# Starting a layer's first products on half of its row tiles, and moving turned tiles between PSUM banks

## The reference

```python
for i in range(DEPTH):                       # block 2, DEPTH = 2
    last = i == DEPTH - 1
    hx = rmsnorm_2(x, g_pre_mix[i]) * (1.0 + sc1) + sh1
    hc = rmsnorm_2(ctx, g_pre_mix[i]) * (1.0 + csc1) + csh1
    px = hx @ w_in[i]                        # q, k, v, Fourier part, 3 Hyena parts
    pc = hc @ (w_in[i][:, K0:F0] if last else w_in[i])
    ...                                      # attention of q over [kc, k], [vc, v]
    hy_x = hyena_mix(px[..., H0:], w_hy_conv[i], b_hy_conv[i], filt, hy_bias[i])
    mix_x = jnp.concatenate([attn_x, four_x, hy_x], axis=-1) @ w_out[i]
    x = x + ga1 * rmsnorm_2(mix_x, g_post_mix[i])
    ...                                      # the same for ctx, only if not last
    fx = rmsnorm_2(x, g_pre_ffn[i]) * (1.0 + sc2) + sh2
    x = x + ga2 * rmsnorm_2(conv_ffn_2(fx, ...), g_post_ffn[i])
    ...                                      # the same for ctx, only if not last
```

## Time and profile before

| | us |
|---|---|
| median of 3 runs | 1617.51 (1617.08 to 1620.24) |
| the profiled execution, its own time | 1620.15 |
| its span in the trace | 1618.3 |
| granted clock of TensorE, mean | 0.996 |
| PE busy | 1573.3 |
| DVE busy | 1114.7 |
| ACT busy | 832.2 |
| POOL busy | 276.6 |

### The profile page before, as it was taken

How to read it: one execution, slowest core, us unless ns; L and a number is a source line. 1 busy time by engine, 2 the same in 40 slices (tenths; PEclk the granted TensorE clock), 3 DMA queues, 4 the chain that set the end, 5 groups by cost and what they waited for, 6 DMA issues and landing times.

```text
span 1618.3 us, 22543 instructions
## 1 busy us (share of the span) xinstructions
PE 1573.3 (97%) x8459; PEld 1270.3 (78%) x8459; DVE 1114.7 (69%) x1830; ACT 832.2 (51%) x1524; POOL 276.6 (17%) x336
## 2 busy tenths in 40 slices
PE   8999999999999999999989999999999999999998
PEld 7667888887677888878857788888888886788886
DVE  5686899656877999755775745444533587689974
ACT  5556666545555666542355533333411544667653
POOL 2000011810003111900010001111272001001163
PEclk9999999999999999999999999999999999999999
DMA  8556866555579654652264433332232346656652
GB/s 274 182 175 194 225 188 182 188 185 169 192 259 255 172 157 156 207 183 85 79 244 122 138 109 93 104 102 82 103 131 97 101 147 207 174 154 183 191 197 80
DMA packets 267349, 261.72 MB, mean 162 GB/s; under 512 B 9025, under 2 KB 209009, under 8 KB 266602
## 3 DMA queue, kind: packets, MB, share of 16 engines
q1 hardware_dynamic: 262986, 246.15, 49.6%
q0 software_dynamic: 3968, 13.82, 2.5%
q10 hardware_dynamic: 288, 0.33, 0.1%
HBM read 259.12 MB, written 1.13 MB: 161 GB/s over the span
## 4 chain that ended last, share of the span: by engine, by line
PE 81%; DVE 11%; ACT 4%; DMA 2%; issue 2%; SPq 0%; DVEq 0%; ACTq 0%
PE psv L584 58%; PE pss L584 20%; DVE wL L1368 2%; PE pss L634 2%; DMA ring<-in_w_up 1%; ACT scr L2206 1%; PE psv L634 1%; ACT wH L2063 1%; DVE scr L1564 1%; DVE hHL L1439 1%; DMA ring<-in_w_in 1%; DVE scr L1565 1%; DVE mx L1530 1%; ACT scr L2063 0%; DVE W L1430 0%
## 5 line engine op out<-in xcount | busy, mean ns | idle before, releaser
L584 PE MATMUL psv<-hHL,wH 128*128 128x512 f32 (+1 forms) x1952 | 641.1, 391 | 6.5 <-DVE hHL L1439 3.4
L1368 DVE TENSOR_TENSOR wL<-ring,wH 128x1024 fp32r<-128x1024 f32 (+2 forms) x364 | 454.9, 1254 | 212.4 <-ACT wH L2063 209.4
L2063 ACT ACTIVATE wH<-ring 128x1024 fp32r<-128x1024 f32 (+2 forms) x364 | 377.0, 1040 | 256.0 <-PE psv L584 200.8
L584 PE MATMUL psv<-hHL,wL 128*128 128x256 f32 (+1 forms) x1504 | 466.3, 310 | 0.0
L584 PEld LDWEIGHTS psv<-hHL,wH 128*128 128x128 f32 x1952 | 364.0, 188 | 91.6 <-DVE wL L1368 7.5
L584 PE MATMUL psv<-wH,hHL 128*128 128x512 f32 (+3 forms) x872 | 293.4, 386 | 4.8 <-DVE wL L1368 2.5
L584 PEld LDWEIGHTS psv<-hHL,wL 128*128 128x128 f32 x1504 | 284.5, 189 | 15.7
L584 PE MATMUL pss<-wH,hHL 128*128 128x512 f32 (+3 forms) x872 | 291.6, 384 | 1.3 <-ACT scr L2063 1.0
L584 PEld LDWEIGHTS psv<-wH,hHL 128*128 128x128 f32 x872 | 162.9, 188 | 43.0 <-DVE wL L1368 9.3
L584 PEld LDWEIGHTS pss<-wH,hHL 128*128 128x128 f32 x872 | 163.0, 188 | 34.3 <-issue 2.3
L1157 POOL TENSOR_TENSOR W<-scr 128x256 f32<-128x256 f32 (+1 forms) x88 | 82.4, 937 | 563.2 <-ACT scr L2268 563.2
(11 more groups left out here) (280 smaller groups left out, 1606.0 us busy)
## 6 DMA issues: line engine op xcount, KB each, us to landing
ring<-in_w_up SPq DMA_DIRECT2D x176, 512.0 KB, 5.2
ring<-in_w_mod SPq DMA_DIRECT2D x96, 512.0 KB, 4.8
ring<-in_w_down SPq DMA_DIRECT2D x88, 512.0 KB, 4.3
ring<-in_w_in SPq DMA_DIRECT2D x52, 512.0 KB, 4.6
ring<-in_w_out SPq DMA_DIRECT2D x32, 512.0 KB, 5.1
ring<-in_w_in SPq DMA_DIRECT2D x8, 384.0 KB, 6.1
W<-gate_scratch POOLq DMA_DIRECT2D x3, 1024.0 KB, 7.6
ring<-in_w_in SPq DMA_DIRECT2D x8, 288.0 KB, 6.6
```

The source lines that it names most:

```text
L584: return pe.matmul(o, a, b, start=start, stop=stop, skip_group_check=True)
L1368: v.tensor_tensor(lo, raw, hi.bitcast(F32), ALU.subtract).then_inc(piece_split, told("piece_split", p))
L2063: return ac.activation(o, i, ACT.Copy)
```

## The change

There are three parts.

**The context follows later.** At the end of block 2's first layer `transition()` gives way to `context_later()`, on DVE and on ACT. Only tiles 0 and 1 are brought to the end before the Hyena pieces. Tile 0 is turned inside the last down products of tile 3, tile 1 right behind them; there is no `keep_clock`. The residuals and the normalising of tiles 2 and 3, their squares, their turns and parts, and the modulation column run between the Hyena pieces (`context_features`, `context_squares`). The context's gain row has a tile of its own, `gain_ctx`, that POOL loads with one DMA of 512 KB.

**pT in the V banks.** In block 2's attention the turned probabilities go to PSV instead of PSS. ACT and DVE get waits that keep the order of the rotation.

**By halves.** All V halves of the low parts are made first, then all S halves, so that the next products can begin with the V half's features while the S halves are still made; ACT makes the high parts in a matching order. One tile before each product stage (tile 1, or tile 3 before the first layer's FFN of block 2) is normalised in two operations of 512, and its V half is turned after the first. In the two-tile transition the first weight split stands ahead of tile 1's gate.

```diff
@@ -640 +646 @@
+    def normalised(ph, t, k0):
+        if t == halved(ph) and k0 == 0:
+            pe.wait_ge(rows_normalised, at("rows_normalised", ph, t, "half"))
+        else:
+            pe.wait_ge(rows_normalised, at("rows_normalised", ph, t))
     def feature_tile(ph, t, x, banks=None):
...
-        pe.wait_ge(rows_normalised, at("rows_normalised", ph, t))
         for (kind, b), k0 in zip(banks or feature_banks(ph, t), (0, 4)):
+            normalised(ph, t, k0)
             for k in range(4):
@@ -777 +791 @@
                 two = (2 * p - 4, 2 * p - 3)
-                pe.wait_ge(S_free, at("S_free", ph, "pT", two[1]))
+                pe.wait_ge(FREE[turned], at(turned + "_free", ph, "pT", two[1]))
                 b = open_("V", ph, "pv", two[1])
@@ -789 +803 @@
                     pe.wait_ge(probs_ready, at("probs_ready", ph, i))
-                    transposes("S", (ph, "pT", i), [(probs(i)[:, c * P:(c + 1) * P], slice(c * P, c * P + P)) for c in range(4)])
+                    transposes(turned, (ph, "pT", i), [(probs(i)[:, c * P:(c + 1) * P], slice(c * P, c * P + P)) for c in range(4)])
             if p - 1 in mods:
@@ -901 +915 @@
             kind = "VS"[t % 2]
+            if (ph, t, h, j) == (("b2", 0), 3, 1, NJ - PIECES):
+                feature_tile(("b2", 1, "mix"), 0, xn4[:, 0, :])
             if j == 0:
@@ -1000 +1016 @@
         pe.wait_ge(pick_made, 5)
-        to_features2(ph + ("mix",), range(4 if l else NT), MOD2[l - 1]["end"] if l else MOD2[l]["start"], (0, 6, 0, 2) if l else (0, 4))
+        if last:
+            feature_tile(ph + ("mix",), 1, xn4[:, 1, :])
+            modulation_row(1, MOD2[0]["end"][0], "S")
+        else:
+            to_features2(ph + ("mix",), range(NT), MOD2[l]["start"], (0, 4))
         def hyena_columns(s):
@@ -1026 +1046 @@
-        for m in HY:
-            tile_split(ntok, ph, "hy", m, head=(ph + ("mix",), 3 if l else 1) if m == HY[0] else None)
+        for i, m in enumerate(HY):
+            tile_split(ntok, ph, "hy", m, head=(ph + ("mix",), 1) if m == HY[0] else None)
+            if last and i == 0:
+                modulation_col(1, MOD2[0]["end"][0], "S")
             if m == 0:
...
                     hyena_columns(s)
+            if last and i >= 4:
+                feature_tile(ph + ("mix",), i - 2, xn4[:, i - 2, :])
         hyena_forward(0)
@@ -1038 +1062 @@
             hyena_forward(1)
+        if last:
+            pe.wait_ge(V_free, at("V_free", ph + ("mix",), "hT", 3))
+            pe.wait_ge(S_free, at("S_free", ph + ("mix",), "hT", 3))
         project_split(range(4), [512] * nt + [256] * (4 - nt), (ph, "kvf"))
@@ -1426 +1456 @@
         inverse1(t)
-        v.wait_ge(gain_rows_in, at("gain_rows_in", ph[1], ph[2]))
-        v.scalar_tensor_tensor(x, xs[:, t, :], rr[:, t:t + 1], gain_rows[:, t // 2, :], ALU.mult, ALU.mult).then_inc(rows_normalised, told("rows_normalised", ph, t))
-    def low_features2(ph, t, cs=()):
+        ctx_ = ph == ("b2", 1, "mix") and t >= 2
+        if ctx_:
+            v.wait_ge(context_gain_in, at("context_gain_in", "all"))
+        else:
+            v.wait_ge(gain_rows_in, at("gain_rows_in", ph[1], ph[2]))
+        if ctx_:
+            v.scalar_tensor_tensor(x, xs[:, t, :], rr[:, t:t + 1], gain_ctx, ALU.mult, ALU.mult).then_inc(rows_normalised, told("rows_normalised", ph, t))
+        elif t == halved(ph):
+            v.scalar_tensor_tensor(x[:, 0:512], xs[:, t, 0:512], rr[:, t:t + 1], gain_rows[:, t // 2, 0:512], ALU.mult, ALU.mult).then_inc(rows_normalised, told("rows_normalised", ph, t, "half"))
+            v.scalar_tensor_tensor(x[:, 512:D], xs[:, t, 512:D], rr[:, t:t + 1], gain_rows[:, t // 2, 512:D], ALU.mult, ALU.mult).then_inc(rows_normalised, told("rows_normalised", ph, t))
+        else:
+            v.scalar_tensor_tensor(x, xs[:, t, :], rr[:, t:t + 1], gain_rows[:, t // 2, :], ALU.mult, ALU.mult).then_inc(rows_normalised, told("rows_normalised", ph, t))
+    def low_features2(ph, t, cs=(), parts=(0, 4)):
...
         c = slice(t * P, (t + 1) * P)
-        for kind, k0 in (("V", 0), ("S", 4)):
+        for k0 in parts:
+            kind = "VS"[k0 // 4]
             v.wait_ge(feat_high, at("feat_high", ph, t, k0))
@@ -1445 +1486 @@
                 normalise2(nph, t - 2, xn4[:, t - 2, :])
+            if nt == 2 and t == 1:
+                splits_to(first, 0)
             for h in range(1 if what == "out" else 0, 2):
@@ -1452 +1495 @@
         normalise2(nph, nt - 1, xn4[:, nt - 1, :])
-        if nt == 2:
-            splits_to(first, 0)
         for c in cs[:-1]:
             modulation_col(1, c)
-        for t in range(nt):
-            low_features2(nph, t, cs)
-            if t == 1:
-                for c in cs[-1:]:
-                    modulation_col(1, c)
+        for k0 in (0, 4):
+            for t in range(nt):
+                low_features2(nph, t, cs, (k0,))
+                if t == 1 and k0 == 0:
+                    for c in cs[-1:]:
+                        modulation_col(1, c)
+    def context_later(ph, nph, first):
+        for t in range(NT):
+            for h in range(2):
+                gate_half(ph, "down", "ffn", t, h)
+            residual(ph, "down", "ffn", t)
+        normalise2(nph, 0, xn4[:, 0, :])
+        gate_half(ph, "down", "ffn", 2, 0)
+        normalise2(nph, 1, xn4[:, 1, :])
+        gate_half(ph, "down", "ffn", 2, 1)
+        gate_half(ph, "down", "ffn", 3, 0)
+        low_features2(nph, 0, (), (0,))
+        splits_to(first, 0)
+        gate_half(ph, "down", "ffn", 3, 1)
+        low_features2(nph, 1, (), (0,))
+        low_features2(nph, 0, (), (4,))
+        low_features2(nph, 1, (), (4,))
@@ -1551 +1615 @@
                 splits_to(early[0], p - early[1][0])
+            if ph[0] == "b2" and 1 <= p <= n and (p in mods or p - 1 in mods):
+                v.wait_ge(V_free, at("V_free", ph, "pT", 2 * p - 1))
             if p - 1 in mods:
@@ -1935 +2002 @@
+        def context_features(i):
+            nph, row = ph + ("mix",), MOD2[0]["end"][0]
+            if i == 0:
+                modulation_col(1, row)
+                residual(("b2", 0), "down", "ffn", 3)
+            if i in (1, 2):
+                normalise2(nph, i + 1, xn4[:, i + 1, :])
+            if i >= 4:
+                low_features2(nph, i - 2, (row,))
         for i, m in enumerate(HY):
             splits_to(first_piece[ph, "hy"] + i)
+            if last and i == 0:
+                residual(("b2", 0), "down", "ffn", 2)
             v.wait_ge(V_full, at("V_full", ph, "hy", m))
@@ -1964 +2044 @@
                     v.tensor_copy(uT[s].rearrange("p t c -> p (t c)"), bank("V", ph, "uT", s)).then_inc(V_free, told("V_free", ph, "uT", s))
+            if last:
+                context_features(i)
         v.wait_ge(V_free, at("V_free", ph, "hy", 1))
@@ -2150 +2232 @@
         norm(nt - 1)
-        for t in range(nt):
-            high_features2(nph, t)
-    def high_features2(ph, t):
+        for t, k0 in ((0, 0), (0, 4), (1, 0), (1, 4)) if nt == 2 else ((0, 0), (1, 0), (0, 4), (2, 0), (1, 4), (3, 0), (2, 4), (3, 4)):
+            high_features2(nph, t, (k0,))
+    def context_later(ph, nph, first):
+        for t in range(NT):
+            for h in range(2):
+                post_half(ph, "down", "ffn", t, h)
+        context_squares(ph, nph, 0)
+        post_half(ph, "down", "ffn", 2, 0)
+        context_squares(ph, nph, 1)
+        post_half(ph, "down", "ffn", 2, 1)
+        post_half(ph, "down", "ffn", 3, 0)
+        high_features2(nph, 0)
+        splits_to(first, 0)
+        post_half(ph, "down", "ffn", 3, 1)
+        high_features2(nph, 1)
+        row = MOD2[0]["end"][0]
+        ac.wait_ge(S_free, at("S_free", nph, "hT", 1))
+        ac.wait_ge(S_full, at("S_full", "modrow", 1, row))
+        copy(mrow[:, :], bank("S", "modrow", 1, row)).then_inc(S_free, mark("S_free", "modrow", 1, row))
+    def context_squares(ph, nph, t):
+        ac.wait_ge(residual_updated, at("residual_updated", ph, "ffn", t))
+        sumsq(xs[:, t, :], D, t, nph, t)
+    def high_features2(ph, t, parts=(0, 4)):
...
         c = slice(t * P, (t + 1) * P)
-        for kind, k0 in (("V", 0), ("S", 4)):
+        for k0 in parts:
+            kind = "VS"[k0 // 4]
             ac.wait_ge(FULL[kind], at(kind + "_full", ph, "hT", t))
@@ -2212 +2320 @@
                     ac.wait_ge(V_full, at("V_full", ph, "pv", (j - 4) | 1))
-                ac.wait_ge(S_full, at("S_full", ph, "pT", j))
-                copy(pT(j), bank("S", ph, "pT", j)).then_inc(S_free, mark("S_free", ph, "pT", j))
+                ac.wait_ge(FULL[turned], at(turned + "_full", ph, "pT", j))
+                if turned == "V":
+                    ac.wait_ge(V_free, at("V_free", ph, "pv", 2 * p - 3) if p >= 2 else at("V_free", "modrow", 1, row))
+                copy(pT(j), bank(turned, ph, "pT", j)).then_inc(FREE[turned], mark(turned + "_free", ph, "pT", j))
             if p in early[1]:
@@ -2425 +2535 @@
```

(20 more changed lines are left out.)

24 lines of the change are left out of this document (17 added, 7 removed).

## The result

| | before | after | ratio, 95% interval |
|---|---|---|---|
| first comparison, us | 1617.51 (4 runs) | 1609.15 (1608.44 to 1609.83, 4 runs) | 0.9944 (0.9933 to 0.9956) |
| second, us | 1618.56 (13 runs) | 1613.35 (1610.52 to 1615.95, 8 runs) | 0.9967 (0.9955 to 0.9978) |
| third, us | 1618.63 (13 runs) | 1615.00 (1611.84 to 1616.44, 9 runs) | 0.9973 (0.9963 to 0.9983) |

The change makes the kernel faster, by .3 to .6 per cent. The ratio, which weighs all executions, gives 9.1 us there; in the two later comparisons of the same two kernels it gives 5.3 and 4.4. Why the first comparison gives so much more than the other two is a part of what follows.

A forecast was written before the change was run, and what follows sets the result against it. PE, busy 97%, bounds the kernel, so only its gaps and useless work can yield. Stage 1.3, banks 1.9, halves 3.2 make 6.4, less 1.7 for the clock: 4.7, so 1612.8 us; own range 1610.8 to 1614.8, wider 1609.5 to 1617.5.

The forecast's parts named there:

- block 1: first FFN, second mix, second FFN: Halved normalise shortens PE's waits for normalised tiles in block 1: .46 and .25 us, nothing before the second FFN.
- before block 2's first mix: Halved normalise takes .6 us off PE's wait of 1.1 before block 2's first mix.
- block 2's first attention: Turned probabilities in the V banks let scores start earlier in the first layer's attention: 1.2 us gained.
- before its FFN: Before the FFN of block 2's first layer, S parts go behind V halves and PE's wait goes: 1.44 us.
- the stage with the context later: From block 2's first-layer down products to `hyena_forward`: starts 1.1 to 1.5 us earlier, taken as 1.3.
- the clock behind the new wait: PE's new wait of about 3.5 us ahead of `x1 * v` drops the clock, 3 in 4: 1.7 us lost.
- PE's side and DVE's side of the stage: PE alone would start `hyena_forward` 6.2 us earlier; DVE's list decides, PE waits some 5.5, leaving 1.3.
- The V banks: In block 2's attentions, scores stop waiting for exponentials but copies still hold value products: 1.9 us, range 0 to 4.4.
- pair steps: First attention: .3 us at the start, .18 in each of three iterations from maxima's earlier start, .4 at the end.
- rival A: The clock holds behind the new wait, so the whole 6.4 us is gained: 1611.1 us; chance .20.
- B: Halves and banks bring a fifth, 1.0 us; with 1.3 less 1.7, .6 gained: 1616.9 us; chance .27.
- C: DVE's and ACT's context work is not hidden at all: 5.7 us slower, 1623.2 us; chance .08.

The follow-up runs named there:

- split_first: Changed kernel with ACT's high part of the second Hyena weight piece ahead of the modulation row's copy; median 1611.50 us, ratio 0.9956 to the kernel before.
- order_later: `split_first` plus, on DVE, tile 3's normalise behind `x1 * v` and q's third weight split earlier; median 1609.55 us, ratio 0.9946 to the kernel before.
- keep_three: Changed kernel with 9, 7 and 7 `keep_clock` products in three PE waits in both blocks; median 1612.47 us, ratio 0.9961 to the kernel before.
- only_halves: Changed kernel with the four-tile `transition` and the S banks kept, so only the halves remain; ratio 0.9980 to the kernel before, 3.2 us.
- only_banks: Kernel before with only the turned probabilities moved to the V banks; ratio 0.9989 to the kernel before, 1.8 us.
- best_of_all: `order_later`'s order, `keep_three`'s places with 9, 7, 7, and 4 more `keep_clock` products at two further waits; median 1609.51 us, ratio 0.9944 to the kernel before.
- best_fitted: `best_of_all` with its `keep_clock` products cut to 5, 4, 3, 2 and 2 to fit the waits; median 1607.41 us, ratio 0.9935 to the kernel before.

## Why the prediction was right or wrong

Step by step, in the pair of profiles whose FFN products run alike (the second of before, the first of after):

| step | predicted | measured |
|---|---|---|
| block 1: first FFN, second mix, second FFN | .46, .25, 0 | .25, .12, 0 (.4 won, given back at weights) |
| before block 2's first mix | .6 | .4 |
| block 2's first attention | 1.2 | 2.1 |
| before its FFN | 1.4 | 1.4 |
| the stage with the context later | 1.3 | 1.2 |
| second attention | .7 | .8 |
| before the last FFN | .45 | .2 |
| sum (shifts under .2 between the places left out above) | 6.4 | 6.5 |
| the clock behind the new wait | -1.7 | 0 in this pair |

The step that failed is the clock term, -1.7, for a fall behind the new wait. In the profile of the first comparison it was 0, and by their mean clock its four executions lost no more than the kernel before does. That leaves the steps' 6.4. The 8.4 measured is 2.0 beyond them; no step of the kernel is known for these, and their cause stays open.

- **PE's side and DVE's side of the stage** were right, and so was the point that 6.2 us of freed PE time bring a fifth of that: PE waited .85, .83 and 3.18, where 1.0, 1.2 and 3.5 were said. DVE's list sets the end; `split_first` and `order_later` shorten that list and the stage shortens with it.
- **The V banks**: the waits for exponentials went and turned into waits for copies, as said. The first attention gave .9 more than forecast. Which of its pair steps was mis-sized no run separates.
- **The clock** was the term that failed in the comparison that counts. The prediction charged 1.7 for a fall. In the profile the clock held, and the four executions had a mean granted clock of .9970, no lower than the kernel before has in any set (.9966 to .9969). So 6.4 was left, rival A's 1611.1. That is rival A by mechanism, but not for its reason: "the gap of 2.11 did nothing" held for one execution only, and in the next profile of the kernel before the same gap brought the clock down. The first profile, too, held a longer fall that the prediction passed over, behind a wait of 2.51 that ended at 426.94: windows of .50 and .66 from 428 on. In the 17 later executions the charge was there: .0016 to .0018 of clock is 2.6 to 2.9 us of work.
- **What a fall costs.** It costs less time than the work that is lost by it, or none: 1.7 lost ahead of `hyena_forward` cost 1.6, 3.4 lost there cost 2.6 and 2.8, 1.7 at block 2's first attention 1.6 (98.98 against 97.42 in the two profiles of before), and 1.7 in block 1's second attention nothing (142.34 us with it, 142.41 without, from the modulation row ahead of the mix to the next). Of six profiles with the wait of 3.2 the clock fell in four. In the five with the stage unchanged, the stage took 28.75, 28.70, 31.30, 31.54 and 30.36 (`keep_three`): on the mean 1.4 above the lowest. So 1.7 was a fair mean for something that happens or not in one execution.
- **The last 2.0 us.** "I take the gain from the profiled one and subtract it from the median" did no harm by its start: later medians of the kernel before are 1615.88 to 1618.63, around the 1617.51. What lay low were the four executions of after, 1608.4 to 1609.8, below all 17 later ones (the lowest is 1610.52). Their better clock is worth up to 3.2 us against those. A second part can be the pace. Each of the two 256-column FFNs runs in one of two paces, 2.3 us apart, in kernels of every order. The first profile of after had both fast, the later two had one and two slow; over all 14 profiles both were fast in three, the first was slow in three and the second in eleven. The other three of those four executions have no profile, so their pace is not known. The forecast gave one number for an execution and had no term for this spread. With the 17 later executions the gain is 4.4 to 5.3, on the forecast's 4.7, which holds a clock term of 1.7 where some 2.6 of work was lost: the sum came out right, and its terms only roughly.
- **Rivals B and C** fell. B wanted 1.0 from halves and banks together: `only_halves` alone gave 3.2 (at least 1.8), and the attention of `only_banks` is 1.9 shorter. C fell since the context's work did hide, all but 1.7 us of waits for weights and the 3.2.

What stays open: what chooses the pace of the FFN products, and why the four executions of the first comparison lost less to the clock (.996 to .998) than most of the later 17 (.993 to .997). No run here changes either on purpose, and whether the chip that a set ran on has a part in it was not tested.

## What to carry to other kernels

When work is moved under products to fill an idle engine, add up that engine's list over the stage: here DVE's 3.2 us of slack and 3.5 us more of PE's useful work settled that 6 us of removed dummy products would bring 1.2. Before a difference of half a per cent is explained, profile the old kernel twice: 5.5 us separated two executions of the same program, and the comparison of four runs was some 4 us off. And look at the mean granted clock of every execution, not of the profiled one alone: here it showed in which sets the clock's part of the gain was missing, which no single profile did.

## What the runs showed of the hardware

- PE's products with full clock and no idle time ran in two paces, 228 to 229 or 232 to 233 instructions in 40 us, for a whole FFN stage, in kernels of every order; the other, wider FFN kept one pace (178 to 179).
- The same wait does or does not bring the clock down: waits of 3.18 and 3.19 left it at 1.00 twice and brought it to half rate for 3.4 or 6.8 us four times. A wait of 1.40 did it once (at 514.84). The wait of 2.5 in block 1's second attention did it in nine of eleven profiles, that of 1.9 to 2.1 at the start of block 2's first attention in nine of eleven.
- With all these waits filled (`best_of_all`, `best_fitted`) there was no half rate before the end in the two profiles, and the mean granted clock was .999 or more in each of the eleven executions. With the wait ahead of the turn down from 3.2 to 1.3 (`order_later`) the mean rose from .9950 to .9970.
- The Trainium skill, "TensorE: Matmul & The Clock Gate", section "Why this matters for your kernels", says that gaps between bursts bring the clock down. Of the six waits of 3.2 the traces agree in four. The page speaks of gaps longer than the 1.76 and 2.11 that the prediction set beside it, so these two are no test of it; but falls behind waits of 1.4, 1.9 and 2.5 came all the same.
- An f32 product of `keep_clock` with 256 columns takes .46 us in two rows (18 rows in 4.15 us).
